# Two heads at a time in the hosted attention stage, and scores put ahead of the up-sums on TensorE

## The reference

```python
def fox_attention(q, k, v, log_f):      # 8 heads of 64, causal over all keys
    ...
    s = jnp.einsum('bqhd,bkhd->bhqk', q_i, k) * scale
    s = s + (c_i[..., :, None] - c[..., None, :])       # c: running sum of log_f
    p = jax.nn.softmax(jnp.where(causal, s, NEG_INF), axis=-1)
# swa_attention: 8 heads of 64 over 2 key groups, own and previous block of 128 keys,
#   alibi bias, one more logit per head (the sink) in the softmax
# memory_attention: 4 heads of 128 over 256 memory rows, no mask, no bias
```

## Time and profile before

| quantity | value |
|---|---|
| median of the runs | 3985.33 us |
| profiled execution, its time | 3991.26 us |
| its span | 3989.4 us |
| PE busy | 3057.4 us (77%) |
| DVE busy | 2370.5 us (59%) |
| ACT busy | 915.4 us (23%) |
| POOL busy | 1152.4 us (29%) |
| attention stage, first half | 1779.0 to 1948.7 us |
| attention stage, second half | 2674.1 to 2860.3 us |

### The profile page before, as it was taken

How to read it: one execution, slowest core, us unless ns; L and a number is a source line. 1 busy time by engine, 2 the same in 40 slices (tenths; PEclk the granted TensorE clock), 3 DMA queues, 4 the chain that set the end, 5 groups by cost and what they waited for, 6 DMA issues and landing times. The chain is left out here.

```text
span 3989.4 us, 51160 instructions
## 1 busy us (share of the span) xinstructions
PE 3057.4 (77%) x18686; PEld 1577.7 (40%) x18686; DVE 2370.5 (59%) x6158; ACT 915.4 (23%) x2506; POOL 1152.4 (29%) x1029
## 2 busy tenths in 40 slices
PE   5975596756787765988899865979798876676666
PEld 4853395612354211633455522634465531111111
DVE  6557745476446677457545577457645578655554
ACT  2113232012111112136321111136412111111111
POOL 0000000043333444323323342323333334444442
PEclk8998698867798876977999986969999987766666
DMA  5510002289999999988999997977999999999998
GB/s 214 188 68 1 6 4 93 97 364 400 350 384 372 419 411 393 400 322 309 367 398 373 370 406 269 411 286 264 348 416 376 360 398 395 413 419 417 420 420 354
DMA packets 207064, 1263.90 MB, mean 317 GB/s; under 512 B 25748, under 2 KB 28948, under 8 KB 72356
## 3 DMA queue, kind: packets, MB, share of 16 engines
q0 software_dynamic: 147456, 1073.81, 67.3%
q1 hardware_dynamic: 59368, 186.95, 12.6%
HBM read 1256.17 MB, written 4.46 MB: 316 GB/s over the span
## 5 line engine op out<-in xcount | busy, mean ns | idle before, releaser
L243 POOL DMA_INDIRECT held_z<-in_experts,held_expert x512 | 579.0, 1131 | 1274.6 <-PE held_acc L263 907.6
L263 PE MATMUL held_acc<-held_z,held_diag 64*64 64x512 f32 x4096 | 697.6, 775 | 286.8 <-ACT held_diag L289 262.9
L263 PE MATMUL held_acc<-held_pair,held_diag 64*64 64x512 f32 x4096 | 688.9, 768 | 253.8 <-ACT held_diag L289 248.9
L243 POOL DMA_INDIRECT held_pair<-in_experts,held_expert x512 | 569.6, 1112 | 1047.6 <-PE held_acc L263 971.4
L309 DVE CUSTOM_DVE_ANT_0 held_z<-held_z,held_hrow 128x1024 f32<-128x1024 f32 x512 | 625.5, 1223 | 377.4 <-DMA held_z<-in_experts,held_expert 371.1
L309 DVE CUSTOM_DVE_ANT_0 held_pair<-held_pair,held_hrow 128x1024 f32<-128x1024 f32 x512 | 625.4, 1223 | 369.3 <-DMA held_pair<-in_experts,held_expert 360.7
L289 ACT ACTIVATE held_diag<-held_bands,held_weight 128x64 f32<-128x64 f32 x1024 | 347.7, 340 | 1467.7 <-DVE held_weight L304 1434.3
L263 PEld LDWEIGHTS held_acc<-held_z,held_diag 64*64 64x64 f32 x4096 | 135.2, 157 | 693.3 <-ACT held_diag L289 566.4
L263 PEld LDWEIGHTS held_acc<-held_pair,held_diag 64*64 64x64 f32 x4096 | 134.3, 155 | 670.4 <-ACT held_diag L289 570.8
L282 ACT ACTIVATE held_bent<-held_dot 128x2 f32<-128x2 f32 x512 | 104.0, 203 | 716.1 <-DVE held_dot L309 688.7
L1773 PE MATMUL c_ps<-held_hT,c_w 128*128 128x256 f32 x640 | 151.9, 392 | 0.0
(11 more groups left out here) (499 smaller groups left out, 4038.8 us busy)
## 6 DMA issues: line engine op xcount, KB each, us to landing
pgh_w<-in_w_in SPq DMA_DIRECT2D x38, 512.0 KB
p2h_w<-in_w_in SPq DMA_DIRECT2D x36, 512.0 KB
p_raw<-in_w_in SPq DMA_DIRECT2D x34, 512.0 KB, 3.5
p_w_ada<-in_w_ada SPq DMA_DIRECT2D x16, 1024.0 KB, 6.1
c_w<-in_w_query SPq DMA_DIRECT2D x20, 512.0 KB, 3.2
held_z<-in_w_in SPq DMA_DIRECT2D x20, 512.0 KB
c_w<-in_w_peer_q SPq DMA_DIRECT2D x20, 512.0 KB
ada_w<-in_w_ada SPq DMA_DIRECT2D x4, 2048.0 KB, 18.7
```

The lines of the kernel that those rows point to most:

```text
L243: pool.indirect_dma_start(self.pair[m % BUFS], None, self.layers[t // TT][0], bass.IndirectOffsetOnAxis(ap=self.expert[:, t % TT, s:s + 1] ...
L263: last = pe.matmul(self.sum_of(i)[to * BAND:(to + 1) * BAND], diag[band, :], up[band, turn * WIDE:(turn + 1) * WIDE], start=s == 0, stop=s ...
```

## The change

In `attention_stage` TensorE issues `score(0)` ahead of the loop and `score(step + 1)` behind `weigh_values(step - 3)` and ahead of the beats. The second mixer gets a stage of its own, `pair_attention_stage`, with items that hold one or two heads: fox keeps one head an item (16 items), sliding attention has pairs (8 items), memory attention too (4 items). That is 28 items and 32 points.

```diff
+                score(0)
                 for step in range(N + 4):
-                    if step < N:
-                        score(step)
                     if 2 <= step < N + 2:
                         turn(step - 2)
                     if 3 <= step < N + 3:
                         weigh_values(step - 3)
+                    if step + 1 < N:
+                        score(step + 1)
                     beats.pe(pe, step)
```

The new stage, cut to what differs from the old:

```diff
+def pair_attention_stage(nc, name, k, items, beats, spare, late_from, loads=(), late_loads=(), sink_loads=(), saves=(), fetch=None):
+    ps, pt = r.ps("ps", (P, 2, 512)), [r.ps(f"pt{u}") for u in range(2)]
+    po = r.ps("po")
+    scores = lambda n: ps[:, :, 0:items[n].width] if items[n].apart else by_head(ps[:, n % 2, :], n)
...
+                def weigh_values(n):
+                    pe.wait_ge(copied, n + 1)
+                    if n:
+                        pe.wait_ge(taken, n)
...
+                for step in range(N + 4):            # ScalarE
+                        for o in range(items[n].count):
+                            ins = act.activation(by_head(p[n % 3], n)[:, o, :], scores(n)[:, o, :], ACT.Exp, bias=nmax[:, m:m + 1],
+                                                 accum_out=total[:, m:m + 1])
+                        ins.then_inc(exped, 1)
+                        if sunken(n):
+                            act.activation(esink[:, sink_cols(n)], esink[:, sink_cols(n)], ACT.Exp).then_inc(sunk, 1)
+                        act.activation(pT[n % 2][:, 0:items[n].wide], pt[n % 2][:, 0:items[n].wide], ACT.Copy).then_inc(copied, 1)
...
+                def peak(n):                         # VectorE, one instruction each for both heads
+                        link.announce(dve.tensor_tensor(part, part, it.bias, ALU.add), biased, masked[0])
+                    link(dve.reduce_max(nmax[:, cols(n)], got, AX))
+                    if sunken(n):
+                        link(dve.tensor_tensor(nmax[:, cols(n)], nmax[:, cols(n)], it.sinks, ALU.max))
+                        dve.tensor_tensor(esink[:, sink_cols(n)], it.sinks, nmax[:, cols(n)], ALU.subtract)
+                    dve.tensor_scalar(nmax[:, cols(n)], nmax[:, cols(n)], -1.0, None, ALU.mult).then_inc(maxed, 1)
...
+                for step in range(N + 4):            # VectorE
+                    if 4 <= step:
+                        take(step - 4)
+                    if step < N:
+                        peak(step)
+                    if 1 <= step <= N:
+                        weigh(step - 1)
+                    beats.dve(dve, step)
```

More of the change, by code:

```diff
@@ L2085, in second_mixer @@
             a = Room(nc, fox, own("fox"))
-            lanes = lambda head: slice(head % 2 * 64, head % 2 * 64 + 2)
+            lanes = lambda o: slice(o * 64, o * 64 + 2)
             items = []
+            both = lambda ap, count: bcast(ap, count, 1)
+            half_rows = [slice(0, FD), slice(FD, P)]
             for c in range(FH // 2):
[L2089 to L2093, removed]
+                for t in tiles:
+                    for some in ([0], [1]):
+                        part = [half_rows[o] for o in some]
+                        pair = [(z[half_rows[o], Y_FQ + c, here(t)], fox_k[half_rows[o], c, 0:(t + 1) * P],
+                                 (fq[lanes(o), c, here(t)], fk[lanes(o), c, 0:(t + 1) * P])) for o in some]
+                        rows = None if len(some) == 2 else part[0]
+                        items.append(Item(pair, both(k.causal[:], len(some)), [[v[:, c, j, half_rows[o]] for j in range(t + 1)] for o in some],
+                                          [(half_rows[o], 0) for o in some], foxT[rows if rows is not None else slice(0, P), c, here(t)], rows=rows, apart=len(some) == 2))
@@ L2094, in second_mixer @@
             kept = [(fox_k[:, :, 0:HALF], past.fox_k), (swa_k[:, 0:HALF], past.swa_k), (v[:, :, 0:HTILES, :], past.v)]
             alibi, sinks = a.sb("alibi", [P, SH, 2 * P]), a.sb("sinks", [P, SH])
[L2096 to L2100, removed]
+            for c in range(SH // 2):
+                part = half_rows[2 * c // (SH // SG)]
+                for t in tiles:
@@ L2101, in second_mixer @@
                     k0 = max(t - 1, 0)
-                    items.append((z[part, Y_SQ + head % 4, here(t)], swa_k[part, k0 * P:(t + 1) * P],
-                                  alibi[:, head, (0 if t else P):2 * P], [v[:, 4, j, part] for j in range(k0, t + 1)], head, t - first, None))
-            sunk_to = len(items)
+                    pair = [(z[part, Y_SQ + head % 4, here(t)], swa_k[part, k0 * P:(t + 1) * P], None) for head in (2 * c, 2 * c + 1)]
+                    items.append(Item(pair, alibi[:, 2 * c:2 * c + 2, (0 if t else P):2 * P], [[v[:, 4, j, part] for j in range(k0, t + 1)]] * 2,
+                                      [(half_rows[o], 0) for o in range(2)], swaT[:, c, here(t)], sinks=sinks[:, 2 * c:2 * c + 2]))
@@ L2105, in second_mixer @@
+            late_from = len(items)
             mkv = z[:, Y_FK:Y_SQ, :]
-            items += [(z[:, Y_MQ + head, here(t)], mkv[:, head, :], None, [mkv[:, 4 + head, j * P:(j + 1) * P] for j in range(2)], head, t - first, None)
-                      for head in range(GH) for t in tiles]
-            spare = [room[:, c:c + 2, :].rearrange("p a n -> p (a n)") for c in (Y_SKV, Y_FF, 3 * DC + 4, 3 * DC + 6)]
[L2109 to L2113, removed]
+            for c in range(GH // 2):
+                for t in tiles:
+                    pair = [(z[:, Y_MQ + head, here(t)], mkv[:, head, :], None) for head in (2 * c, 2 * c + 1)]
+                    items.append(Item(pair, None, [[mkv[:, 4 + head, j * P:(j + 1) * P] for j in range(2)] for head in (2 * c, 2 * c + 1)],
+                                      [(slice(0, P), o) for o in range(2)], memT[:, 2 * c:2 * c + 2, here(t)], whole=True))
@@ new lines, in second_mixer @@
+            spare = [room[:, c:c + 2, :].rearrange("p a n -> p (a n)") for c in (Y_SKV, Y_FF, 3 * DC + 4, 3 * DC + 6)]
+            pair_attention_stage(nc, own("foxa"), k, items, beats["attention"], spare, late_from, late_loads=[(mkv, memory)],
+                                 fetch=lambda sp: first_tile.fetch(sp, ins["w_in_2"][Y_GATE:Y_N]),
+                                 sink_loads=[(alibi[:], ins["alibi"]), (sinks[:], ins["swa_sinks"].to_broadcast([P, SH]))],
+                                 loads=kept if half else [], saves=[] if half else [(there, here_) for here_, there in kept])
```

126 lines of the change are left out of this document (added).

## The result

The changed kernel takes 3947.7 us in the median of four runs (3944.27 to 3951.37), the kernel before 3984.64 us beside it on the same chip. The ratio is 0.9898, with a 95% interval of 0.9875 to 0.9922: 1.0% faster. The forecast was 3954.

What follows compares the result with a forecast made beforehand. In the two attention stages TensorE bounds fox items, mutual waits the sliding ones, the DMA's pace memory and drain. 153.5 and 171.0 us against 169.7 and 186.2, -31.4 from 3991.3 gives 3959.9, less 5.9: 3954, range 3928 to 3983.

Steps and rivals of the forecast that it cites:

- Sliding, memory and drain: Attention stages: sliding parts fall to 40 and 42 us from 60.9 and 62.6, memory with drain to 36.5 each.
- the wide bias: VectorE's 512-wide bias add for a pair, absent from the trace: taken as 0.70 us, between bounds 0.428 and 0.856.
- The `taken` wait at nothing: TensorE's values for an item now wait for VectorE's take of the item before: priced at 0 us.
- the first of the two reasons given: For the free `taken` wait: VectorE now does the take first in its point.
- the second reason: For the free `taken` wait: behind the waiting TensorE stand only the next score and up-sums needed one point later.
- The upper bound of 1.2 us a point: Most the `taken` wait could cost, from memory attention's 4 waits of 4.9 us in the first half.
- 8 slots more on the engine that is full: Fox parts, TensorE: slots rise from 17 to 25, adding 12.6 and 10.6 us; parts become 77 and 92.5 us.
- where TensorE is full (fox), that gives nothing: Scores ahead of up-sums in fox parts: only swaps the order of work that all has to be done; no gain.
- rival A: Faster: fewer TensorE holes earn more full clock; stages 145.5 and 161.5 us, -49, kernel 3936; chance 0.20.
- fox would get the clock of its neighbours: Fox parts, within rival A: mean clocks become 0.83 and 0.89 for 0.69 and 0.82.
- Rival C: Slower: TensorE's clock falls to 0.66 with more bursts of two up-sums, net +19, kernel 4004; chance 0.09.
- The signs: Right if stages near 154 and 171 us, fox longer by some 10, sliding shorter by 20, VectorE's score waits under 10.

Runs made afterwards that it cites:

- e1: Kernel before with only TensorE's scores moved ahead of the up-sums (single heads, 40 items, 44 points, old waits): 3965.19 us, ratio 0.9935.
- e7: Changed kernel with VectorE's bias, maximum, sum, reciprocal and take done once for each head inside the pairs: 3962.64 us, ratio 0.9942.
- e9: Changed kernel, but where successive fox heads write different partitions TensorE waits only for the take before the last: 3946.45 us, ratio 0.9892.
- e3: Changed kernel with VectorE's take put last in its point, the stricter output wait kept: 3965.36 us, ratio 0.9944.
- e2: Changed kernel with the scores behind the up-sums again in the pair stage: 3979.24 us, ratio 0.9973.
- e10: The kernel before, unchanged, run once more for a second trace: 3984.72 us, ratio 0.9991.
- e0: The changed kernel, unaltered, run once more for a second trace: 3944.72 us, ratio 0.9887.
- e11: Kernel before with scores ahead and VectorE's take first in its point; single heads, old waits: 3953.37 us, ratio 0.9905.
- e4: Changed kernel with the 50 slots dealt to the kinds of item as before the change: 3959.25 us, ratio 0.9922.
- e5: Changed kernel with slots dealt by price, second half 30 fox, 12 sliding, 6 memory, 2 drain: 3944.55 us, ratio 0.9893.
- e6: Changed kernel with two fox heads in one item in the first half alone (24 points): 3936.24 us, ratio 0.9869.
- e8: Changed kernel with e6's fox pairs in the first half and e5's shares in the second: 3942.41 us, ratio 0.9888.

## Why the prediction was right, and which term was off

| part, us | forecast | changed kernel | once more |
|---|---|---|---|
| fox, first half | 77 | 72.1 | 65.2 |
| fox, second half | 92.5 | 78.9 | 79.3 |
| sliding | 40, 42 | 40.0, 43.3 | 39.1, 43.6 |
| memory and drain | 36.5, 36.5 | 37.0, 37.3 | 37.0, 36.8 |
| stages | 153.5, 171.0 | 149.1, 159.5 | 141.3, 159.7 |

**Sliding, memory and drain: right in length, and by VectorE's steps.** VectorE came out as priced, 34.7 and 36.7 us for 36 and 37, with the wide bias at 0.690 us for 0.70. TensorE did not: after the slots moved out it was to keep 41.5 and 44.7 us, and it had 33.6 and 37.4, at clocks no higher than those assumed (0.79 and 0.84 for 0.83 and 0.89). The forecast put at nothing what pairs save on TensorE. The product with the values, at the full clock, for one head before and for a pair after:

```profile
2791.70 0.65 PE L929 MATMUL foxah_po<-held_z,partsh_v 128*64 128x128 f32 x4 [0.25 <-ACT held_z L965]
2758.07 0.66 PE L1106 MATMUL foxah_po<-foxah_p,partsh_v 128*64 128x128 f32 x8
```

Eight passes, which alternate between the two heads and their two halves of the partitions, take as long as four passes of one head. Busy time times mean clock, an estimate of the work in us of the full clock, fell from 114.4 to 103.9 over the first stage and from 142.6 to 131.9 over the second, with the same number of groups; e1, with single heads, still has 114 and 143. So the two savings come together, and for the second half's sliding part e7 shows that VectorE's is the smaller one: there only 1.6 us came back. No run here separates TensorE's saving from the smaller number of points. The last part's 37 us, at a share of 0.97, are what its bytes ask for.

**The `taken` wait at nothing: right, by the first of the two reasons given.** e9 shows that the strict wait costs nothing that can be told, e3 that it costs some 20 us once the take is last. So it is the take's place that does it; that "only the next score and the up-sums" stand behind the waiting TensorE, the second reason, holds in e3 too and did not help. The upper bound of 1.2 us a point was near the 1.06 of e3.

**Fox: the direction was off in the second half, and two terms did it.** The first is "8 slots more on the engine that is full". I read 17 slots off GpSimd's DMAs. The 16 fox points hold 50 x 16 / 44 = 18 slots, and TensorE runs one up-sum a slot, so it was 7 more. Two of these lie behind the part's end in the new order. Passes of L263 in the second half's fox part, before:

```profile
L263 PE MATMUL held_acc<-held_pair,held_diag 64*64 64x512 f32 x80 | 14.9, 827 | 0.7 <-ACT held_diag L289 0.7
L263 PE MATMUL held_acc<-held_z,held_diag 64*64 64x512 f32 x64 | 8.7, 614 | 0.0
```

and after:

```profile
L263 PE MATMUL held_acc<-held_pair,held_diag 64*64 64x512 f32 x96 | 14.9, 720 | 0.0
L263 PE MATMUL held_acc<-held_z,held_diag 64*64 64x512 f32 x88 | 11.3, 608 | 0.0
```

144 passes became 184, at 8 a slot 18 up-sums became 23 (e2, with the scores behind, has 200 passes, all 25). Five more in the part, not eight: at the forecast's own 1.33 us that is 4 us of its error of 13.6, and 2.7 of these 4 only say where the part is cut.

The second is the clock, which the sum held at 0.82 because "where TensorE is full (fox), that gives nothing". In work of the full clock the part has, before, 81.28 x 0.82 = 66.7, and in e10 83.33 x 0.80 = 66.7. With scores ahead alone, and one up-sum fewer: 77.20 x 0.85 = 65.6. After: 78.86 x 0.90 = 71.0, and in e0 79.30 x 0.89 = 70.6. So five more up-sums cost 4.3 us of full clock, 0.86 each, in line with the 0.91 between the two starts in the timeline; and 71.0 us of work passed in 78.9 us because the clock rose. At 0.82 it would have been 86.6: the clock is worth 8 us. With the 4 of the count that is 12 of 13.6 us, and the rest is that an up-sum more costs 0.86 us and not 1.09.

What the mean clock is made of can be read by stretch. The second half's fox part before (the half-clock stretches alone), then the opening in e1, in the changed kernel and in e7 (columns as in the earlier trace rows):

```profile
2674.10:2699.70 25.60, 25.60 (x61) 7.78 (x62) 10.55 (x28) 11.43 (x21) 3.36 (x4) 0.50 0.55 204
2720.20:2723.60 3.40, 3.40 (x18) 2.04 (x18) 2.97 (x9) 1.59 (x5) 0.00 (x0) 0.51 0.97 366
2659.40:2682.80 23.40, 23.40 (x53) 7.24 (x54) 10.64 (x28) 11.65 (x21) 4.67 (x3) 0.50 0.49 176
2652.60:2668.30 15.70, 15.65 (x36) 4.08 (x36) 8.86 (x23) 8.38 (x15) 2.60 (x2) 0.50 0.49 187
2658.00:2682.90 24.90, 24.90 (x61) 7.53 (x61) 11.70 (x30) 11.26 (x21) 5.53 (x4) 0.50 0.53 195
```

In all fourteen traces TensorE enters this part at the lower level, behind a wait of 7.8 to 9.3 us for partsh_v at the stage's opening, and works at half clock for a while. The mean is above all the length of that stretch. In total the part has 29.0 us at half clock before and 33.3 in e10; 39.5 in e2, which rises after 12.3 us already and then falls back three times; 22.1 to 23.7 in the kernels with scores ahead and single heads or old slots (e1, e11, e4); 15.2 to 16.8 in the changed kernel, e0, e3, e5, e6 and e9; but 23.1 in e8, which falls back once for 6.8, and 24.9 in e7, which has the changed kernel's fox instructions. So the traces separate by the order without overlap, three with 29.0 us or more, eleven with 24.9 or less. The size is uncertain: the same instructions gave 15.7 and 24.9. In the first half the means overlap: 0.69, 0.73 and 0.68 behind, 0.69 to 0.82 ahead. *Why* one trace has more of it than another stays open, and with it whether the order is the cause; TensorE is busy throughout the opening before and in e1, and no run takes the wait in front of it away. Half of rival A (clock up) thus came true, in the second half and by another way than A had it, "fox would get the clock of its neighbours": the neighbours stayed at 0.79 and 0.84. A's stages, 145.5 and 161.5 us, are nearer to the two traces of the changed kernel than the forecast's.

**Rival C did not come.** The stages' clocks are 0.80 and 0.91, where they were 0.81 and 0.88. The page "TensorE: Matmul & The Clock Gate" of the Trainium skill, section "Part 4: PE-mode transpose", spoke for a fall; with transposes and up-sums unchanged in number over the stage, no fall is seen. It neither confirms nor refutes the page, since no run here removes the transposes.

**The sum, and luck in it.** -47.3 us in the stages for -31.4 forecast. The profiled execution, to be 3959.9, took 3945.4: 14.5 us off. The median is only 6.3 off, 3947.7 for 3954, since the forecast had taken off 5.9 us that the profiled execution of before lay above its median, while that of after lay 2.3 *below* its own. So more than half of the error in the stages is hidden by which executions happened to be profiled: in the trace the gain is 45.9 us, in the medians of the same series 36.9 for 31.3 forecast, and in e0's 43.8.

**The signs.** Met were these: sliding parts shorter by 20 us, clocks between 0.75 and 0.92, waits for the output's take under 10 us a half, the next stage moved by 4.2 us only (142.0 for 137.8). Not met: the second stage was not near 171 us, TensorE was busy 129.9 and 145.0 us for "near 141 and 162", VectorE waited 10.2 and 22.2 us for fox scores instead of under 10, and one fox part was not longer, which the prediction had named as a sign of being wrong.

## What to carry to other kernels

"Busy all the time" is not "at its limit": multiply busy time by the granted clock before you say that a reordering on the full engine is worth nothing. Where two pipelines share an in-order engine, put the work that another engine waits for ahead of the block that nobody waits for, and on that other engine put first the copy that frees a buffer. When you count what a part of a stage costs, count the instructions of the engine that bounds it, in that window, and see what a new order moves over the window's edge. When a mean clock differs, look where in the part the low stretch lies before you call it a property of the work.

## What the runs showed of the hardware

- TensorE can work at half clock for long while busy throughout: 25.60 of 25.60 us before and 23.40 of 23.40 in e1, each behind an opening wait of over 8 us; the same instructions had 15.7 us of it in the changed kernel and 24.9 in e7.
- Eight passes that alternate between two heads and their halves of the partitions take 0.66 us, four passes of one head 0.65, both at the full clock.
- The same kernel, part and instructions can have a clock of 0.72 in one execution and 0.82 in another, which is 7 us of 72; the whole execution differed by 6.7 us (3945.4 and 3938.71).
- Two up-sums issued back to back take 1.88 us from the first start to the next matmul's (2709.25 to 2711.13), one alone 1.02 us (2704.63 to 2705.65), both at the full clock: a block of two costs less than two blocks of one.
